# One transfer or two for a tile of expert weights

## The reference

```python
def moe_swiglu(h, router, w_gate, w_up, w_down):
    ...
    logits = (hf @ router).astype(jnp.float32)
    top_val, top_idx = lax.top_k(logits, TOP_K)
    gates = jax.nn.softmax(top_val, axis=-1)
    ...
    def expert_block(inp):
        x_blk, e = inp
        return (jax.nn.silu(x_blk @ w_gate[e]) * (x_blk @ w_up[e])) @ w_down[e]
```

## Time and profile before

| what | value |
|---|---|
| median of 3 runs | 1686.65 us (1686.63 to 1687.36) |
| the profiled execution | 1685.95 us |
| its span, first to last instruction | 1684.2 us |
| TensorE busy | 1575.2 us, 94% of the span |
| VectorE busy | 1277.2 us, 76% |
| ScalarE busy | 1078.4 us, 64% |
| granted TensorE clock, mean | 0.977 |
| moved by DMA | 425.49 MB, mean 253 GB/s |

### The profile page before, as it was taken

One profiled execution on the slowest core, in us unless ns is written; L12 is line 12 of the kernel. 1 busy time (PEld: TensorE's weight loads), 2 busy tenths in 40 slices (PEclk: granted clock), 3 DMA queues, 4 the chain that ended last, 5 costly groups with the idle time before them and its releaser, 6 DMA issues.

```text
span 1684.2 us, 35533 instructions
## 1 busy us (share of the span) xinstructions
PE 1575.2 (94%) x13674; PEld 1429.3 (85%) x13674; DVE 1277.2 (76%) x1746; ACT 1078.4 (64%) x1668; POOL 0.2 (0%) x4
## 2 busy tenths in 40 slices
PE   6987886999999868999999999999999999999996
PEld 6766786999989857898898898998898898998995
DVE  6855326655555865589899899889889889889885
ACT  5653335544445434677777777777777777777774
POOL 0000000000000000000000000000000000000000
PEclk9988998999999988999999999999999999999998
DMA  8002003455544312599999999999999999999992
GB/s 333 8 1 114 4 4 150 154 184 187 187 152 150 113 39 102 195 369 364 345 371 370 345 367 369 339 372 357 349 371 358 348 367 359 351 369 360 355 366 108
DMA packets 71967, 425.49 MB, mean 253 GB/s; under 512 B 8128, under 2 KB 8128, under 8 KB 37712
## 3 DMA queue, kind: packets, MB, share of 16 engines
q1 hardware_dynamic: 71888, 424.38, 67.7%
HBM read 423.30 MB, written 1.05 MB: 252 GB/s over the span
## 4 chain that ended last, share of the span: by engine, by line
PE 58%; DVE 2%; issue 1%; ACT 1%; DVEq 0%; ACTq 0%
PE bank L156 18%; PE bank L158 18%; PE bank L157 18%; PE bank L1804 1%; PE bank L1821 1%; ACT w_high L150 1%; PE bank L1770 1%; DVE w_low L153 1%; DVE more_slots_low L153 0%; PE bank L2060 0%; DVE slots_low L153 0%; DVE scratch L1989 0%; PE bank L1779 0%; DVE scratch L2128 0%; DVE x_tok_low L153 0%
## 5 line engine op out<-in xcount | busy, mean ns | idle before, releaser
L153 DVE TENSOR_TENSOR w_low<-ring,w_high 128x1024 fp32r<-128x1024 f32 x801 | 951.7, 1220 | 133.2 <-ACT w_high L150 133.1
L150 ACT ACTIVATE w_high<-ring 128x1024 fp32r<-128x1024 f32 x801 | 811.1, 1052 | 51.0 <-PE bank L158 41.0
L156 PE MATMUL bank<-w_high,slots_high 128*96 128x256 f32 x896 | 257.3, 287 | 0.3 <-issue 0.3
L156 PE MATMUL bank<-w_high,more_slots_high 128*96 128x256 f32 x896 | 257.2, 287 | 0.0
L158 PE MATMUL bank<-w_high,slots_low 128*96 128x256 f32 x896 | 250.3, 279 | 0.0
L158 PE MATMUL bank<-w_high,more_slots_low 128*96 128x256 f32 x896 | 250.3, 279 | 0.0
L157 PE MATMUL bank<-w_low,more_slots_high 128*96 128x256 f32 x896 | 250.2, 279 | 0.0
L157 PE MATMUL bank<-w_low,slots_high 128*96 128x256 f32 x896 | 250.2, 279 | 0.0
L150 ACT ACTIVATE turned_high<-bank 128x96 fp32r<-128x96 f32 x224 | 56.5, 252 | 234.5 <-PE bank L1804 234.5
L156 PE MATMUL bank<-w_high,turned_high 128*96 128x512 f32 x448 | 176.6, 394 | 0.7 <-DVE turned_low L153 0.7
L158 PE MATMUL bank<-w_high,turned_low 128*96 128x512 f32 x448 | 176.6, 394 | 0.0
(11 more groups left out here) (354 smaller groups left out, 2563.3 us busy)
## 6 DMA issues: line engine op xcount, KB each, us to landing
ring<-in_w_moe SPq DMA_DIRECT2D x224, 1024.0 KB, 7.1
ring<-in_w_moe SPq DMA_DIRECT2D x224, 512.0 KB, 7.2
ring<-in_w_ffn SPq DMA_DIRECT2D x22, 1536.0 KB, 6.6
ring<-in_w_in SPq DMA_DIRECT2D x15, 1536.0 KB, 6.8
ring<-in_w_out SPq DMA_DIRECT2D x6, 1536.0 KB, 7.1
scratch<-in_x SPq DMA_DIRECT2D x2, 512.0 KB, 3.7
out_y<-xn SPq DMA_DIRECT2D x2, 512.0 KB, 3.8
const<-in_const SPq DMA_DIRECT2D x1, 948.0 KB, 12.8
```

The costliest lines, as they stand in the source:

```text
L150: return nc.scalar.activation(dst, src, ACT.Copy)
L153: return nc.vector.tensor_tensor(dst, src, high.bitcast(f32), sub)
L156: nc.tensor.matmul(out, left[0], right[0], start=start, stop=False, **flags)
```

## The change

The front and the back of an expert's tile are brought by one transfer of 1.5 MB. `load_front` and `load_back` become `load_tile`, which waits for `back_split` (all three thirds of the tile four before it are split) and raises `slot_loaded`. `back_loaded` and ScalarE's wait for it are gone. The first four tiles of the experts are brought by one transfer each as well. The loop of `moe_loads` has one issue a tile. What the tiles hold, and all work on ScalarE, VectorE and TensorE, stays as it was.

```diff
--- before.py
+++ after.py
@@ -162,7 +162,6 @@
 
         consts_loaded, rest_loaded, x_loaded = sem("consts_loaded"), sem("rest_loaded"), sem("x_loaded")
         slot_loaded = [sem(f"slot_loaded{i}") for i in range(RING)]
-        back_loaded = [sem(f"back_loaded{i}") for i in range(RING)]
 
         front_high, back_high, front_split, back_split = (sem(n) for n in ("front_high", "back_high", "front_split", "back_split"))
         tile_done = sem("tile_done")
@@ -188,11 +187,7 @@
         def load_group(sp, g, src):
             if g >= RING:
                 sp.wait_ge(back_split, g - RING + 1)
-            if g < G_MOE:
-                sp.dma_start(ring[:, g % RING], src).then_inc(slot_loaded[g % RING], 16)
-            else:
-                sp.dma_start(ring[:, g % RING, 0:2 * D], src[:, 0:2 * D]).then_inc(slot_loaded[g % RING], 16)
-                sp.dma_start(ring[:, g % RING, 2 * D:], src[:, 2 * D:]).then_inc(back_loaded[g % RING], 16)
+            sp.dma_start(ring[:, g % RING], src).then_inc(slot_loaded[g % RING], 16)
 
         IN0_GROUPS = [4, 6, 5, 1, 2, 0, 3]
         IN0_TILES = [(o, n, GROUP * g + n) for o, g in enumerate(IN0_GROUPS) for n in range(GROUP) if GROUP * g + n < 20]
@@ -1632,16 +1627,10 @@
         w_moe = io["w_moe"].rearrange("e t p n -> (e t) p n")
         N_MOE = E * FET
 
-        def load_front(sp, tile, g, split):
-
-            sp.wait_ge(front_split, split)
-            sp.dma_start(ring[:, g % RING, 0:2 * D], w_moe[bass.ds(tile, 1), :, 0:2 * D].rearrange("a p n -> (a p) n"))\
-                .then_inc(slot_loaded[g % RING], 16)
-
-        def load_back(sp, tile, g, split):
+        def load_tile(sp, tile, g, split):
+
             sp.wait_ge(back_split, split)
-            sp.dma_start(ring[:, g % RING, 2 * D:], w_moe[bass.ds(tile, 1), :, 2 * D:].rearrange("a p n -> (a p) n"))\
-                .then_inc(back_loaded[g % RING], 16)
+            sp.dma_start(ring[:, g % RING], w_moe[bass.ds(tile, 1)].rearrange("a p n -> (a p) n")).then_inc(slot_loaded[g % RING], 16)
 
         def front_high_part(act, g, n, turns):
 
@@ -1650,7 +1639,6 @@
             high_part(piece(w_split[0], g % 2, n), piece(ring, g % RING, n)).then_inc(front_high, 1)
 
         def back_high_part(act, g, turns):
-            act.wait_ge(back_loaded[g % RING], (turns + ((g - G_MOE) // RING + 1)) * 16)
             high_part(piece(w_split[0], g % 2, 2), piece(ring, g % RING, 2)).then_inc(back_high, 1)
 
         def front_low_part(dve, g, n, tiles):
@@ -1724,21 +1712,12 @@
 
         def moe_loads(sp, at):
 
-            def turn(i, j):
-                load_front(sp, i * RING + (j + 1), at.g0 + j + 1, i * RING + (at.g0 + j - RING + 2))
-                load_back(sp, i * RING + j, at.g0 + j, i * RING + (at.g0 + j - RING + 1))
-
-            if at.p == 0:
-                for j in range(1, RING):
-                    turn(1, j)
-            else:
-                load_front(sp, 0, at.g0, at.g0 - RING + 1)
-            with sp.Fori(2 if at.p == 0 else 0, N_MOE // RING - 1) as i:
+            for j in range(RING):
+                if at.p or j > 1:
+                    load_tile(sp, j, at.g0 + j, at.g0 + j - RING + 1) if at.p else load_tile(sp, RING + j, at.g0 + j, at.g0 + j + 1)
+            with sp.Fori(1 if at.p else 2, N_MOE // RING) as i:
                 for j in range(RING):
-                    turn(i, j)
-            for j in range(RING - 1):
-                turn(N_MOE // RING - 1, j)
-            load_back(sp, N_MOE - 1, at.g0 + RING - 1, at.g0 + N_MOE - RING)
+                    load_tile(sp, i * RING + j, at.g0 + j, i * RING + (at.g0 + j - RING + 1))
 
         def moe_products(pe, at):
             p, tiles0, e0, g0 = at.p, at.tiles0, at.e0, at.g0
@@ -2042,9 +2021,8 @@
             @block.sync
             def _(sp):
                 load_ahead(sp, G_OUT1, G_MOE)
-                load_front(sp, RING, G_MOE + RING, G_MOE + 1)
-                load_front(sp, RING + 1, G_MOE + RING + 1, G_MOE + 2)
-                load_back(sp, RING, G_MOE + RING, G_MOE + 1)
+                load_tile(sp, RING, G_MOE + RING, G_MOE + 1)
+                load_tile(sp, RING + 1, G_MOE + RING + 1, G_MOE + 2)
                 all_passes(sp, moe_loads)
 
             @block.tensor
```

## The result

The changed kernel took a median of 1731.38 us (1725.35 to 1739.28, 4 runs) against 1687.01 us of the kernel before in the same runs: ratio 1.0269, 95% interval 1.0239 to 1.0299. The direction was forecast, the size was not: 44 us in place of 15, and the median lies over the range's upper end of 1725 us. The profiled execution took 1727.77 us, 41.8 us more than that of before.

What follows compares the result with a forecast made beforehand. TensorE was taken to bound the experts' stage, with transfers just keeping up. A stall of 0.07 us over 218 tiles gives 15 us, and 1685.95 + 15 = 1701 us; the range was 1684 to 1725 us.

Steps and rivals of the forecast that it cites:

- TensorE is the bound, and no transfer is waited for; at most 2 us to gain: Experts' stage, 705 to 1640 us: TensorE busy 932.93 of 935.00 us, so only 2.07 us of idle time to gain.
- The window of 7.0 us and the bound of 8.0: Experts' tiles: 7.0 us from issue to use; with 1.03 us of slack, landing within 8.0 us costs nothing.
- the two that the forecast added up: Slack from a late split to TensorE: 1.03 us by ScalarE, 1.10 us by VectorE; the smaller counted.
- The 0.43 us in the forecast's sum for VectorE: VectorE's idle time before 1205.14, counted as slack in 0.46 + 0.43 + 0.21 = 1.10 us.
- Pieces don't matter, the late issue does: Experts' loads: fewer pieces gain little, the bytes being the same; the front leaving 5.42 us later is the certain cost.
- The landing of 8.3 us at a turn of 4.29: Experts' stage: a whole 1.5 MB tile lands 8.3 us after its one issue, from 1.13 + 7.2 us.
- a formula in which 0.1 us of landing is worth 11 us of time: Experts' turn longer by z: window 8.0 + 2z set equal to the landing, 8.3 - 3.2z, over 218 tiles.
- The landing shrinks by 3.2 us per us of turn: Experts' stage: landing falls from 8.3 us at 4.29 to 7.2 at 4.63, giving z = 0.058 us, taken as 0.07.
- one pair of transfers at 630 us: Front and back at 630.28 and 630.66, 4.63 us after another pair, took 7.2 us; used for the slope.
- a small stall in most turns: The forecast itself, experts' stage: 0.07 us a turn, 15 us in all, 1690 to 1712 us, chance 0.47.
- The queue doesn't drain: Rival, experts' stage: landing stays 8.3 us at any turn; 33 us, 1719 (1740 without ScalarE's slack). Chance 0.18.
- The Trainium skill's rule of one DMA, not several: Rule for DMA-bound transfers; by it no loss, 1686 us. The forecast set against it that nothing waits for DMA.

Runs made afterwards that it cites:

- e1_sooner: Changed kernel, but a tile's last third is split ahead of the next tile's second third, so its one transfer leaves 1.13 us sooner: 1688.49 us, ratio 1.0021.
- e3_two_late_both: Changed kernel with 1 MB and 0.5 MB transfers, both issued where its one was, and ScalarE waiting for both before splitting the first third: 1737.83 us, ratio 1.0312.
- e4_before_both: Kernel before, fronts still leaving early, with only ScalarE's wait for both front and back before splitting the first third added: 1687.83 us, ratio 1.0013.
- N = 4: `e1_sooner` with TensorE making each tile's first product four times more (overwritten by the real one), which stretches the turn: 1790.14 us, one run.
- N = 4, 8 and 16: `e1_sooner` with each tile's first product made four, eight or sixteen times more on TensorE: 1790.14, 1891.42 and 2095.53 us, one run each.
- N = 8: `e1_sooner` with TensorE making each tile's first product eight times more (overwritten by the real one), which stretches the turn: 1891.42 us, one run.

## Why the prediction was wrong, point by point

*TensorE is the bound, and no transfer is waited for; at most 2 us to gain.* Right as far as the runs go: no kernel here with whole tiles beat the kernel before.

*The window of 7.0 us and the bound of 8.0.* Right in the number. The stop shown above gives a slack of 1.08 us where the forecast took 1.03, and `e1_sooner` moved the bound by 1.13 us and the loss went with it. But the way to TensorE was another one than the two that the forecast added up: the down product waits for VectorE's lower part of the turned hidden tile (41 times, 20.3 us in the list of waits), with the 0.46 + 0.76 - 0.14 us worked out above. The 0.43 us in the forecast's sum for VectorE stand behind that operation, not ahead of it. That 1.03 comes so near to 1.08 is luck.

*Pieces don't matter, the late issue does.* Right: `e3_two_late_both` has the pieces of before and the loss, `e4_before_both` the early issue and the need of the whole tile, and nearly no loss.

*The landing of 8.3 us at a turn of 4.29.* Right to 0.2 us: 8.5 us in `e1_sooner`, where the turn is unchanged, and 8.4 in the changed kernel. In a formula in which 0.1 us of landing is worth 11 us of time this is a term of its own.

*The landing shrinks by 3.2 us per us of turn.* This step of the sum failed. The slope was drawn from one pair of transfers at 630 us, 4.63 us after a single other pair; such a pair had only one predecessor, while in the stage of the experts every transfer has followed on another for hundreds of turns. The start of the run with N = 4 shows what that makes: 7.3 us behind one predecessor, near the forecast's 7.2, and 8.7 behind two. In the running stage the landing is flat up to 4.75 us, so a longer turn gave nothing back. With a flat landing of 8.4 us the same formula is 8.0 + 2z = 8.4, z = 0.2 us, and 218 x 0.2 = 44 us, where 0.19 us a turn were measured. That it meets the loss so closely is in part luck: the 8.4 us were read after the result, and medians leave the scatter out. The forecast was a small stall in most turns; TensorE's weight loads stopped in 61 of 205, for up to 1.5 us. The flat landing is what the rival "The queue doesn't drain" had, whose own sum of 33 us lacked 0.1 us of landing, as its 8.3 came from the median of split transfers. It, too, was right only up to 4.75 us, as the landing falls at longer turns. The range ended below it because the slope was believed and the rival got 0.18.

*The reason of the flat part.* Open. The rival gave as its reason that DMA engines which fall idle pay a new start. One estimate fits it: at N = 4, 8 and 16 a tile keeps a DMA engine for 4.3 us, 0.6 us more than the 3.7 us that 1.5 MB took right behind another transfer. But the 4.3 us are the same on the flat part and beyond it, so they don't tell why the landing is flat. The runs show that the fill of the turn decides, and that the place of the source and the work of the other engines don't by themselves; what a DMA engine does in the flat part was not tried by itself.

The Trainium skill's rule of one DMA, not several, for a transfer that is bound by DMA ("SBUF — State Buffer", Summary: rules for kernel authors) does not decide this case. Where a whole tile was needed and its transfers left late, one transfer was no worse (1731.38 us against 1737.83 in `e3_two_late_both`, whose second issue leaves later than its first); where the issue was early enough, `e1_sooner` and `e4_before_both`, one transfer and two, differ by 0.7 us in the median (1688.49 and 1687.83). The 44 us come from the moment of the issue.

## What to carry to other kernels

For each transfer compare its landing with the window from issue to use plus the slack behind it; joining two transfers of a slot moves the issue of the first to the release of the last, and that, not the number or size of the transfers, was the price here. Take the landing at the fill that the stage really has, and behind a stream that has run for some turns: here, where the data take 3.7 of 4.29 us, it was 8.5 us, against 6.3 at a turn of 6.15, and it didn't fall when the turn grew to 4.75, so the stall didn't heal itself. If one large transfer is wanted, free its slot sooner first.

## What the runs showed of the hardware

With 1.5 MB per turn on the 16 DMA engines the landing was 8.5 us at a turn of 4.29 us and 8.6 at 4.75, then 7.2 at 5.22 and 6.3 at 6.15; with 1.25 and 1 MB per turn of 4.29 us it was 6.2 and 4.9 us. I had not expected so steep a rise at the same size: from N = 8 to N = 4, a turn shorter by 0.47 us, the landing grows by 1.4 us, and from there to 4.29 us not at all. At the same spacing it took three transfers in a row to get there: 6.2, 7.3 and 8.7 us.
